# Band attention of a streaming encoder: scores in [key, query] tiles, maximum as an added contraction row

## The reference

```python
def band_attend(q, k, v, q_pos, k_pos, rel_bias):
    s = jnp.einsum('bqhd,bkhd->bhqk', q, k).astype(jnp.float32) * C_SCALE
    idx = jnp.clip(q_pos[:, None] - k_pos[None, :], -MAX_REL, MAX_REL) + MAX_REL
    s = s + rel_bias[:, idx].astype(jnp.float32)
    qc = (q_pos // CHUNK)[:, None]
    kc = (k_pos // CHUNK)[None, :]
    valid = (k_pos[None, :] >= 0) & (kc <= qc) & (kc >= qc - LEFT_CHUNKS)
    p = jax.nn.softmax(jnp.where(valid, s, -jnp.inf), axis=-1).astype(v.dtype)
    return jnp.einsum('bhqk,bkhd->bqhd', p, v)
```

## Time and profile before

| | |
|---|---|
| median of three runs | 3708.01 us |
| span of the profiled execution | 3713.2 us |
| instructions | 52940 |
| band stage, first to last exponential | 2171.0 to 2755.9 us |
| first load of the band stage landed, first score | 2157.64, 2166.70 us |

### The profile page before, as it was taken

How to read it: one execution, slowest core, us unless ns; L and a number is a source line. 1 busy time by engine, 2 the same in 40 slices (tenths; PEclk the granted TensorE clock), 3 DMA queues, 4 the chain that set the end, 5 groups by cost and what they waited for, 6 DMA issues and landing times. The chain is left out here.

```text
span 3713.2 us, 52940 instructions
## 1 busy us (share of the span) xinstructions
PE 3417.7 (92%) x20276; PEld 3219.3 (87%) x20276; DVE 1120.3 (30%) x2441; ACT 976.8 (26%) x1858; POOL 779.9 (21%) x450
## 2 busy tenths in 40 slices
PE   6996547998989999999899979999989899999998
PEld 5995427888989999999799968888879899999998
DVE  3112752453131122122311134444431321221223
ACT  3001332553131122121210034444431311211211
POOL 3110011111142232232222100000001522322220
PEclk8997768999999999999999978988889999999999
DMA  3223324221121111110022242332211211111111
GB/s 107 89 92 120 78 83 148 57 54 32 45 69 46 34 56 45 34 46 21 23 76 93 82 114 53 67 61 59 56 42 44 70 46 34 45 56 34 34 34 54
DMA packets 183744, 225.86 MB, mean 61 GB/s; under 512 B 54704, under 2 KB 156289, under 8 KB 183441
## 3 DMA queue, kind: packets, MB, share of 16 engines
q1 hardware_dynamic: 183664, 224.81, 20.6%
HBM read 178.22 MB, written 52.32 MB: 62 GB/s over the span
## 5 line engine op out<-in xcount | busy, mean ns | idle before, releaser
L237 PE MATMUL ffn_banks<-hhi,ffn_whi 128*128 128x384 f32 (+1 forms) x2112 | 692.1, 328 | 18.4 <-POOL hlo L218 13.5
L238 PE MATMUL ffn_banks<-hlo,ffn_whi 128*128 128x384 f32 (+1 forms) x2112 | 691.5, 327 | 0.0
L239 PE MATMUL ffn_banks<-hhi,ffn_wlo 128*128 128x384 f32 (+1 forms) x2112 | 691.4, 327 | 0.0
L237 PEld LDWEIGHTS ffn_banks<-hhi,ffn_whi 128*128 128x128 f32 x2112 | 399.1, 189 | 19.9 <-issue 19.9
L238 PEld LDWEIGHTS ffn_banks<-hlo,ffn_whi 128*128 128x128 f32 x2112 | 399.3, 189 | 0.0
L239 PEld LDWEIGHTS ffn_banks<-hhi,ffn_wlo 128*128 128x128 f32 x2112 | 399.2, 189 | 0.0
L237 PE MATMUL in_banks<-hhi,in_whi 128*128 128x384 f32 (+1 forms) x1104 | 363.2, 329 | 21.6 <-issue 13.6
L891 POOL TENSOR_TENSOR ffn_wlo<-ffn_stage,ffn_whi 128x2048 fp32r<-128x2048 f32 x66 | 303.4, 4610 | 356.3 <-ACT ffn_whi L851 356.2
L238 PE MATMUL in_banks<-hlo,in_whi 128*128 128x384 f32 (+1 forms) x1104 | 362.5, 328 | 0.0
L239 PE MATMUL in_banks<-hhi,in_wlo 128*128 128x384 f32 (+1 forms) x1104 | 362.4, 328 | 0.0
L957 DVE TENSOR_TENSOR ffn_act<-ffn_silu,ffn_banks 128x384 f32<-128x384 f32 x132 | 70.0, 532 | 961.5 <-PE ffn_banks L239 945.1
(11 more groups left out here) (295 smaller groups left out, 5482.8 us busy)
## 6 DMA issues: line engine op xcount, KB each, us to landing
park_z<-in_rows SPq DMA_DIRECT2D x46, 544.0 KB
ffn_stage<-in_w_gate SPq DMA_DIRECT2D x22, 1024.0 KB
ffn_stage<-in_w_up SPq DMA_DIRECT2D x22, 1024.0 KB
ffn_stage<-in_w_down SPq DMA_DIRECT2D x22, 1024.0 KB, 4.9
in_stage<-in_w_qkv SPq DMA_DIRECT2D x12, 1024.0 KB
in_stage<-in_w_in SPq DMA_DIRECT2D x11, 1024.0 KB
band_q_in<-park_z SPq DMA_DIRECT2D x32, 272.0 KB
band_k_in<-park_z SPq DMA_DIRECT2D x32, 272.0 KB
```

The costliest lines, as they stand in the source:

```text
L237: nc.tensor.matmul(out, whi[:, k, :], hhi[:, k, c0:c0 + w], start=(k == 0), stop=False)
L238: nc.tensor.matmul(out, whi[:, k, :], hlo[:, k, c0:c0 + w], start=False, stop=False)
L239: last = nc.tensor.matmul(out, wlo[:, k, :], hhi[:, k, c0:c0 + w], start=False, stop=(k == kts - 1))
```

## The change

The stage is written anew for scores in [key, query] tiles: keys in the partitions, queries in the columns, so that exp's result is what the product with V needs, without a transposition.

- **Pieces.** A head has 13: `BLOCKS` lists key tiles per block of 512 queries, 4 pieces of 512, 384, 256, 128 columns, 8 of 512, 512, 384, 384, 256, 256, 128, 128, and one for the sample with five key tiles x 64 columns.
- **Maximum.** A maximum over keys cannot be taken along partitions. `peak` makes each [query, key] tile once more, in one pass q2 x k2 with the bias once (`near`, float32r) and the mask, into `pM`; DVE takes the maximum. `rows` transposes it to a row, ACT copies it into row 64 of `q3`, and row 64 of `k3` is ones: so `score` subtracts it within the 65-row product k3 x q3 (k low x q high besides). The row maximum is thus of a rounded score; numerator and sum use the same one.
- **Sums.** `V` holds ones where zeros were, so that `weigh` gives the numerator in one half of `pO` and the sum of p in the other. ACT copies out the numerator, DVE the sum, per block of queries; per pair of heads DVE takes the reciprocal and multiplies, ACT and POOL split the result.
- **Preparation** of k2, q3, k3 and the transposed bias goes to POOL (`prepare`). SP loads eleven transfers a head, and a new step on SP at the end of the latent attention, `turn_bias`, writes the bias table reversed and spread as `biasT`.
- The loop over pairs is written out: 16 heads, no hardware loop.

```diff
+def turn_bias(nc, sp, D, bias_in):
+    rel, n = D["rel"], D["rel"].shape[1]
+    back = bass.AP(rel.tensor, n - 1, [[n, C_HEADS], [-1, n]])
+    sp.dma_start(D["relT"], back, allow_slow_non_contiguous=True).then_inc(bias_in, 16)
+    sp.wait_ge(bias_in, 16)
+    rows = bass.AP(D["relT"].tensor, P - 1, [[n, C_HEADS], [-1, P], [1, 2 * P]])
+    sp.dma_start(D["biasT"], rows).then_inc(bias_in, 16)
+    sp.wait_ge(bias_in, 32)
...
+            def peak(h, t):
...
+                pe.wait_ge(s["maxed"], NT * h + t)
...
+                    parts = [(out[:, c:c + kw], q2[:, e, qs], k2[:, e, k0:k0 + kw])]
+                    if i == 0 and 4 <= t < NT - 1:
+                        parts.append((out[:, c:c + CHUNK], halves[0:1, P:2 * P], halves[0:1, 2 * P:2 * P + CHUNK]))
...
+                        parts.append((out[:, lo_:hi_], ident[:], near[:, e, b:b + hi_ - lo_]))
...
+            def rows(h, r):
...
+                else:
+                    if h + 1 < C_HEADS:
+                        pe.wait_ge(s["v_taken"], h + 2)
+                    pe.wait_ge(s["row_kept"], 3 * h + 2)
+                    pe.wait_ge(s["maxed"], NT * h + 9)
...
+                    ins = nc.tensor.transpose(spare[0:1, q * P:q * P + w], neg_max[0:w, e, t:t + 1], S["ident"][0:w, 0:w])
...
+            def score(h, i):
...
+                    parts = [(cols, k2[:, e, keys], q2[:, e, qs]), (cols, k3[:, e, keys], q3[:, e, qs])]
+                    b0 = q0 - j * P
+                    if b0 < 2 * P:
+                        bw = min(w, 2 * P - b0)
+                        parts += [(slice(0, bw), ident[:], biasT[:, e, part, b0:b0 + bw]) for part in range(2)]
+                    if q0 + w == (j + 5) * P:
+                        parts.append((slice(w - CHUNK, w), halves[0:1, 0:P], halves[0:1, 2 * P:2 * P + CHUNK]))
...
+            def weigh(h, i):
...
+                    ins = nc.tensor.matmul(pO[:, G % 2, q0:q0 + w], V[:, e, j, :], p[:, g % RING, 0:w],
+                                           start=(j == BLOCKS[b][0]), stop=(j == BLOCKS[b][-1]))
...
-            def turn(hp, m):
...
-                    ins = nc.tensor.matmul(pP[0:kw, b * P:b * P + w], p[0:w, m % 2, c:c + kw], diag[0:w, m % 2, 0:w],
-                                           start=True, stop=True)
...
+            def divide(pair, t):
...
+                dve.reciprocal(tot[:, cols], tot[:, cols]).then_inc(s["inverted"], 1)
...
+                dve.tensor_tensor(num[:, cols], num[:, cols], tot[:, cols], ALU.mult).then_inc(s["quotient"], 1)
...
+            def prepare(h):
...
+                pool.tensor_copy(k2[:, e, 0:T], k_in[:]).then_inc(s["k_hi"], 1)
+                pool.tensor_scalar(near[:, e, :], b_in[:], b_in[:, 0:1], None, ALU.subtract).then_inc(s["near_set"], 1)
+                pool.tensor_scalar(q3[0:H, e, :], q_in[0:H, :], C_SCALE, None, ALU.mult).then_inc(s["q_low_rows"], 1)
...
+                pool.tensor_tensor(k3[0:H, e, 0:T], k_in[0:H, :], k2[0:H, e, 0:T], ALU.subtract).then_inc(s["k_lo"], 1)
```

More of the change, by code:

```diff
@@ L1730, in band_stage @@
+        num, tot = st.sb("num", [P, T]), st.sb("tot", [P, T])
         halves = st.sb("halves", [1, 2 * P + CHUNK], F32R)
[L1731 to L1737, removed]
+        pS = st.ps("pS", [P, RING, HALF])
@@ L1806, in _ @@
         def _(pe):
[L1807 to L1822, removed]
-                else:
[L1824 to L1840, removed]
+            def turn_v(h):
+                pe.wait_ge(s["loaded"], 16 * LOADS * (h + 1))
+                if h:
+                    pe.wait_ge(s["row_kept"], 3 * (h - 1) + 2)
+                for c in range(8):
+                    ins = nc.tensor.transpose(spare[:, c * H:(c + 1) * H], v_in[:, c * P:(c + 1) * P], S["ident"][0:H, 0:H])
+                ins.then_inc(s["v_turned"], 1)
@@ L1889, in steps @@
-            def steps(hp, first, last):
-                for m in range(2 * N):
-                    if not (last and m == 2 * N - 1):
-                        score(hp, m + 1)
-                    turn(hp, m)
-                    if not (first and m == 0):
-                        weigh(hp, m - 1)
-                    if m % N in STAGE_AT and not (last and m >= N):
-                        turn_in(2 * hp + m // N + 1, STAGE_AT[m % N])
-            for which in range(TURNS):
-                turn_in(0, which)
@@ L1985, in _ @@
[L1985 to L1995 removed]
+                if h >= 2:
+                    act.wait_ge(s["scored"], N * (h - 1))
+                act.activation(q2[:, h % 2, 0:T], q_in[:], ACT.Copy, scale=C_SCALE).then_inc(s["q_hi"], 1)
@@ L2079, in _, with take_v @@
-            set_bias(0, 0)
-            split_q(0, 0)
-            split_bias(0, 0)
-            for which in range(TURNS):
-                take(0, 0, which)
-            maximum(0, 0)
-            inverse(0, 0)
-            steps(0, True, False)
-            with dve.Fori(1, pairs - 1) as hp:
-                steps(hp, False, False)
-            steps(pairs - 1, False, True)
-            low(pairs - 1, 2 * N - 1)
+            def take_v(h):
+                e = h % 2
+                dve.wait_ge(s["v_turned"], h + 1)
+                if h >= 2:
+                    dve.wait_ge(s["summed"], N * (h - 1))
+                    dve.wait_ge(s["stored"], 16 * STORES * (h - 1))
+                dve.tensor_copy(V[:, e, 0:8, own(e)], spare[:].rearrange("p (c n) -> p c n", n=H)).then_inc(s["v_taken"], 1)
@@ L2110, in build @@
+            for t in range(4, NT):
+                low(C_HEADS // 2 - 1, t)
 def build(nc, D):
```

564 lines of the change are left out of this document (329 added, 235 removed).

## The result

The changed kernel takes 3592.3 us (median of four runs, 3590.25 to 3595.75), the kernel before 3703.2 us in the same session; the ratio is 0.970, with an interval of 0.9675 to 0.972. The direction was right; the size was not.

What follows compares the result with a forecast made beforehand. PE was taken to bound the band stage, at a mean clock of 0.85. From the profiled span, 3713.2 - 37 (16 heads) + 8 (ends) = 3684 us; from the median the forecast is 3679 us, range 3612 to 3747.

Steps and rivals of the forecast that it cites:

- The bound and PE's work: Band stage: PE is the limit, and its work per head falls from 30.5 to 25.4 full-clock us.
- The 65-row products: Rival in the k3 score products: 65 contraction rows restart like 64-row ones, 6.8 us a head more, 3807 us; chance 0.03.
- at 0.85 that is 34.5: Band stage: a head's 29.3 full-clock us divided by today's mean clock gives 34.5 us, 2.3 less than now.
- The rival with a higher clock: Band stage: longer streams and fewer switches raise the clock to 0.92, a head takes 31.8 us, 3636 us; chance 0.15.
- its lower end, 3612: Higher clock in the band stage with waits of 2.5 instead of 3.9 us a head, 24 us more gained.
- The waits: PE per head, for takes of v and k and for maxima: 2, 1 and 0.9 us, together 3.9, bounds 0.7 to 7.2.
- the wait for maxima: PE's `peak` has one buffer and waits for the maximum before: 0.9 us a head taken, bounds 0.2 to 1.5.
- The ends: Band stage's start (some 10 us of peaks and maxima) and end (6 us of quotients): 8 us lost net, bounds 0 and 16.
- The 8 us saved on the first and last head: First head needs no transposes of p, the last prepares no next head: saves about 8 of the ends' 16 us.
- The quotients: End of the band stage: five quotients follow the last product, 1.2 us each, 6 us together.
- 57 us of cover: SP, end of latent attention: the bias table's transfer stays off the path unless it takes over 50 us.
- VectorE held behind GpSimd: Rival in the band stage: GpSimd's longer operations hold VectorE's split of q, 39.0 us a head, about 3751 us; chance 0.18.

Runs made afterwards that it cites:

- b_sample_last: The kernel before, with the sample's tile moved from fifth to last of a head's nine, same instructions: 3667.7 us, ratio 0.988.
- a_turn: The changed kernel, with the bias table's rearranging on SP held until the latent attention's last values have landed: 3592.3 us, 0.969 of before.
- a_late: The changed kernel, with a head's third rows behind its ninth piece and the transposes of k and cached keys one and two pieces later: 3597.8 us.

## Why the prediction was wrong

- **The bound and PE's work: right.** 25.4 us a head at the full clock was forecast, 25.34 measured. The 65-row products cost no switch of the price taken: eight of 64 columns, alternating 128 and 65 rows, take 2221.96 to 2222.96, 0.125 us each; that rival falls.
- **The step that failed: "at 0.85 that is 34.5".** I carried the clock of the kernel before over to a changed stream of work. The rows before showed PE busy in the half-clock stretches, and I took the 0.85 as a property of the stage. It goes with the order of the work: `b_sample_last` had 0.95 with the same instructions. Why the changed stream gets 0.97 is not shown; no run takes one part of the change back by itself. 29.3 us at 0.85 are 34.5, at 0.97 30.2: 4.3 us a head, some 68 us. The rival with a higher clock had this mechanism, at 0.92 and 3636 us, with a chance of 0.15; even its lower end, 3612, joined it with only part of the smaller waits.
- **The waits: right in kind and place, too large.** 3.9 us a head taken, 2.06 measured: 1.8 us x 16 / 0.97, some 30 us. The sum lies inside its bounds; the wait for maxima, 0.1 a head, lies below its own.
- **The ends: too small.** 16 us gross forecast, 18 + 6 measured. The nine peaks and maxima ran at half clock: 18.5 us from 2172.82 to 2191.28, where 10 were taken from full-clock rows. The 8 us saved on the first and last head would lie inside the 154 and are not measured by themselves. The quotients took 2633.96 to 2639.77, 5.8 us, as forecast.
- **`turn_bias`: wrong.** "57 us of cover" looked at its end, and not at the loads it shares the queues with. The latent attention lengthened by 8 us in the profiled execution; `a_turn` shows no gain in the time from undoing it.
- **VectorE held behind GpSimd: not in the changed kernel.** GpSimd is busy 166 us in the steady part, 10.5 a head as forecast, but the split of q takes 1.29 us at the median and 1.43 at most. In 14 heads it runs beside GpSimd's one-input multiplication of 2.96 us, and neither is held. A collision in the opening went the other way:

```profile
2168.40 1.29 DVE L2080 SCALAR_TENSOR_TENSOR band_q<-band_q_in,band_q 64x1088 fp32r<-64x1088 f32 x1 [6.53 <-ACT band_q L1988]
...
2168.44 2.05 POOL L2158 TENSOR_SCALAR band_near<-band_b_in 128x256 fp32r<-128x256 f32 x1
...
L2158 POOL TENSOR_SCALAR band_near<-band_b_in x16: 929/932/2046, 2168.4 to 2587.0; 128x256 fp32r<-128x256 f32 x16
...
2309.98 1.29 DVE L2080 SCALAR_TENSOR_TENSOR band_q<-band_q_in,band_q 64x1088 fp32r<-64x1088 f32 x1 [2.63 <-ACT band_q L1988]
...
2308.10 2.97 POOL L2159 TENSOR_SCALAR band_q<-band_q_in 64x1088 fp32r<-64x1088 f32 x1
...
L2080 DVE SCALAR_TENSOR_TENSOR band_q<-band_q_in,band_q x16: 1289/1289/1427, 2168.4 to 2589.8; 64x1088 fp32r<-64x1088 f32 x16
```

In the opening VectorE's split took its usual 1.29 us, and GpSimd's operation, begun just behind it, 2.05 instead of 0.93. In `a_late` GpSimd's two-input operation came first, and the split took up to 3.44 us in three heads: there the rival was real, and cost PE 7.5 us. The Trainium skill, page "SBUF — State Buffer", section "SBUF: two separate sides", says that whichever of the two starts first keeps the shared pair of ports for its whole instruction. The opening and `a_late` agree with it; the 14 heads beside the one-input operation do not. So the rival turns on which operation of GpSimd the split meets, and not on how long GpSimd is busy.

Size of the miss: 68 + 30, less 8 for the ends (24 gross less the 8 taken as saved, where 8 were forecast) and 8 for `turn_bias`, are 82 of 87 us. Beside the changed kernel the kernel before stands at 3703.2 us, 5 us lower than the 3708 from which the forecast starts, and rounding the two clocks to 0.01 alone moves each term by several us, so that the sum is good to no better than that.

## What to carry to other kernels

- Where PE's clock in a stage is not at 1.00, forecast a change with the clock as an unknown of its own, from the present level up to 1.00. In this kernel an edit that changed only the order was worth 44 us net, and one that saved 36 us of PE time gained nothing.
- Judge an edit on PE by its busy time and by the stretch times the granted clock as well as by the time: here one saving came back as a wait (64 full-clock us of work, 22 of the stretch), another was taken by the clock and came out when the waits beside it were moved.
- A transfer put "behind" others on a queue can still slow them: look at what lands next, not only at when it must end itself.

## What was not expected of the hardware

- The granted clock rose from 0.85 to 0.95 with the same instructions in another order, and fell from 0.97 to 0.87 with some 15 us more of waiting.
- Of 16 like heads with the same waits only two or three lost the clock, and not the same ones in each of three traces.
- The clock fell from 0.97 to 0.93 with half the waiting, in `a_late`.
- A 64-row product between 128-row ones cost some 0.27 full-clock us more than one with 128 rows (64 us in 16 heads of 15 such products); 65 rows showed no such price.
- A two-input operation of VectorE was held behind a two-input one of GpSimd (3.28 us instead of 1.29), but not beside a one-input one.
